# Moving the norm factor, the low parts of tile 0 and the state stores at the seams of a ConvFFN phase

## The chip, the cores and the metric

The kernel runs on one core of one Trainium2 chip. The metric is device time in microseconds (us) of one launch; lower is better. TensorE (PE in the rows) multiplies, VectorE (DVE), ScalarE (ACT) and GpSimd (POOL) work element by element, and SyncE (SP) issues every DMA of this kernel.

## What is computed

One inference step of a two-layer causal trunk, for a prompt of 1024 tokens and 8 samples of 4 tokens (T = 1056 columns together), with D = 1024, all in float32. Layer 0 mixes by convolutions, layer 1 by dilated attention; each is followed by the same ConvFFN, twice in all, and the change is in that phase:

```
def conv_ffn(h, st, w_in, wc, w_down):          # h is RMS-normed; D_FF = 2816
    z = h @ w_in                                # 1024 -> 2 * 2816: gate | up
    g, st_new = causal_dwconv(z[..., :D_FF], st, wc)   # width 3
    return (jax.nn.silu(g) * z[..., D_FF:]) @ w_down, st_new
```

The norm factor of a token (1 over the root of its mean square) is not put in the activations before the product: it is a row `rst` of T numbers by which results are multiplied later. The small conv states of layer 0 (`pa_st`, `pb_st`, `AS`, `BS`) are outputs too.

## The kernel before

**Numbers in two parts.** A float32 operand is split in a high part (a copy in fp32r, made by ScalarE) and a low part (the rest, a subtraction); each product is three matmuls (high by high, high by low, low by high). Weights arrive in `w_raw` (three slots of 1024 columns) by `load_unit` from SP.

**The products phase** (`products`, line 942 on; `ffn` of each engine) has 22 tiles j of 128 channels. A tile works on a 2 by 2 block of weights A11, A12 (unit x = 0) and A21, A22 (unit x = 1) with the sums S1 to S4, so that 11 products of 12 matmuls (L950) give gate and up. In TensorE's order they are P1 (A11), G3A, U3A (A21), P5 (S1), P2 (A12), G3B, P6 (S2), P3 (S4), P7 (S3), U3B (A22) and P4. Eight quads of 512 columns (A11, A21, S1, A12, S2, S4, S3, A22) must have both parts in a ring `wq` of six places. Per tile:
- VectorE makes the sums S (`quad_sum`, L2015 to L2023), ScalarE the high parts (`quad_hi`, L1267), GpSimd the low parts (`quad_lo`, L1682);
- ScalarE copies three half-made results out of PSUM (`copy_part` 0, 1, 2, L1281), after P1, P5 and P6; P6, P3 and P7 wait for copies 0, 1 and 2. Copy 1 of tile j also waits for `hidden(j-1)`, whose input it overwrites;
- VectorE adds the pieces (`combine` 0 to 3, L2034 to L2048; the last after P7), scales the gate (`scale_gate`), does the conv (`taps`), ScalarE `silu`, and VectorE `hidden(j)`: three multiplications of up by `sil` (L2094), which stand at the start of tile j+1 and release `prod_ok`.

**The order of queues** is written out by hand and each engine works strictly in it. SP in tile j: `store_hid(j-1)`, which waits for the last of the three multiplications and writes the row to DRAM (`hid_spill`); then `load(base+2*j+3)`, the unit with A21 and A22 of tile j+1; then `load(base+2*j+4)`, with A11 and A12 of tile j+2; in layer 1 and some tiles of layer 0 a 4 MB cache copy. ScalarE in tile j: copy 0, S3, A22, copy 1, A11 and A21 of tile j+1 (A21 waits for its load), copy 2, then S1, A12, S2, S4 of tile j+1, silu(j). GpSimd in tile j: low parts of S3, A22, then of A11, A21, S1, A12 of j+1, `history(j)`, low parts of S2, S4 of j+1; the low part of S2 waits for the sum S4, which VectorE makes after `taps`.

**The start** of the phase (tile 0) also makes the split activations `xo` while the last outputs of the mixer are added to h (L1805); the mean squares are summed in `acc`, spread by TensorE into the PSUM tile `ob`, rooted on ScalarE, and inverted on VectorE (`factor_parts`, L1787). In layer 0 SP issues all ten conv-state stores at j = 0 (L615), between two weight loads and the first hidden store.

**The end and the down phase** (`down_proj`, L806): the hidden rows come back from DRAM in pairs g of 11 (`load_hid`, L595, into `hraw`), GpSimd multiplies each by `rst` (`hidden_scale`, L1703), ScalarE makes the high part (L1478), VectorE the low one (`hidden_lo`, L2099), and TensorE multiplies; two PSUM regions alternate, and VectorE adds each to h. For g+1 both `hidden_lo` stand after the fourth of the eight additions of g.

Of the kernel before, what the change touches and what calls it, by code (L numbers as in the profile page):

```python
# [24 lines left out]
ALU = mybir.AluOpType  # L25
# [168 lines left out]
def build(nc, xT, wstream, par, ident_d, ones_d, stA, stB, stF, kva, kvb, wtab, sbias, cache_k, cache_v,  # L194
# [3 lines left out]
    with ExitStack() as ctx:  # L198
# [41 lines left out]
        AS0 = off  # L240
# [20 lines left out]
        wqr, _ = place("wqr", [P, 6, 2, 512], F32, W1)  # L261

# [38 lines left out]
        ZU = (reg[0][:, 2, 0:TS], ob[:, 1, 0:TS])  # L301

# [55 lines left out]
        hid_out = [sem(f"hid_out{i}") for i in range(2)]  # L358
        hid_in = [sem(f"hid_in{i}") for i in range(2)]
        hr_ok = sem("hr_ok")  # L360
# [33 lines left out]
        def slot_free(eng, L, j, q):  # L394


            n = 8 * j + q
            if n >= 6:
                jj, qq = divmod(n - 6, 8)
                eng.wait_ge(step_full, step_at(L, jj, LAST_STEP[qq]))  # L400
            else:
                for u in range(U_FFN[L] - 3, U_FFN[L]):
                    if u % 3 == ring(L, j, q) // 2:
                        eng.wait_ge(full, LAST[u] + 1)

# [39 lines left out]
        def load_unit(sp, u, slot, i=None, step=3):  # L445

            v = u - 3
            if is_in_unit(v):
# [3 lines left out]
                sp.wait_ge(wq_lo, 8 * (NJ * L + j) + (Q_A22 if x else Q_A12) + 1)  # L452
# [76 lines left out]
        def _(sp):  # L529
# [42 lines left out]
            def ffn_stream(L, last_unit, copies):  # L572
# [8 lines left out]
                def store_hid(j):  # L581
                    sp.wait_ge(prod_ok, 3 * (NJ * L + j + 1))
                    sp.dma_start(hid_d[j], stage[j % 2][:]).then_inc(hid_out[j % 2], 16)

                def load_hid(g):
                    if g >= NG:
                        return
                    for c in range(2):
                        sp.wait_ge(hid_out[c], 16 * (NG * L + g + 1))
# [12 lines left out]
                for j in range(NJ):  # L602
                    if j > 0:
                        store_hid(j - 1)
                    load(base + 2 * j + 3)
                    if j == NJ - 1:
                        load_hid(0)
                    load(base + 2 * j + 4)
                    if L == 0 and j == 0:
# [4 lines left out]
                        for dst, src in states:  # L614
                            sp.dma_start(dst, src).then_inc(st_out, 16)  # L615
# [115 lines left out]
        def _(pe):  # L731
# [203 lines left out]
            def products(L, j):  # L935
# [7 lines left out]
                def product(q, o, out, first, ready):  # L943
                    pe.wait_ge(wq_lo, 8 * jj + q + 1)
# [18 lines left out]
                if j >= 2:  # L963
                    pe.wait_ge(prod_ok, 3 * (jj - 2) + 2)
                product(Q_A21, X_B13, zu, True, lambda k: 3 * k + 2)
# [4 lines left out]
                product(Q_S1, X_T1, ZB, True, lambda k: 3 * k + 3)  # L970
                if j == 0:
# [4 lines left out]
                product(Q_A12, X_B21, ZC, True, lambda k: 12 + 2 * k + 1)  # L976
                product(Q_A12, X_B23, ZG, False, lambda k: 12 + 2 * k + 2)
                if j == 0:
                    pe.wait_ge(std_ok, n - 1)
                    nc.tensor.matmul(ob[:, 0, 0:NS], ones[:, :], acc[:, NP_:], start=True, stop=True).then_inc(st_full, 1)  # L980
# [10 lines left out]
            def ffn(L):  # L991
# [3 lines left out]
                for g in range(NG):  # L995
                    pe.wait_ge(hid_lo, NJ * L + 2 * g + 2)
                    for x in range(2):
                        u = down_unit(L, g, x)
                        down_proj(u, FIRST[u], g % 2, turn=(lambda: pe.wait_ge(prod_ok, 3 * NJ * (L + 1))) if g + x == 0 else None)
# [222 lines left out]
        def _(act):  # L1222
# [28 lines left out]
            def x_sum_hi(L, o, n):  # L1251

                act.wait_ge(xo_raw, 7 * L + n)
                nc.scalar.activation(xo[:, o, 0, :, :], xraw[:, o, 1, :, :], ACT.Copy).then_inc(xo_hi, 1)

            def quad_hi(L, j, q):

                jj = NJ * L + j
                if q in SUM_AT:
                    act.wait_ge(wq_raw, 4 * jj + SUM_AT[q])  # L1260
                    src = wqr[:, ring(L, j, q), 1, :]
                else:
# [20 lines left out]
            def first_tiles(L):  # L1283

                s = (1, 3)[L]
                for m in range(KD):
                    if m % 2 == 0 or L == 1:
                        hi_after(act, U_OUT + 4 + m // 2 if L == 0 else U_WO + m)
                    h_ready(act, s, m)
                    square(s, m, h[:, m, :])  # L1290
                    x_tile(L, m)
                    if m >= 5:
                        quad_hi(L, 0, (Q_A11, Q_A21, Q_S1)[m - 5])
# [6 lines left out]
                x_sum_hi(L, X_T3, 5)  # L1300
# [1201 lines left out]
```

## Time and profile before

| | us |
|---|---|
| median of 3 runs | 2687.76 (2686.51 to 2688.47) |
| the profiled execution: its own time | 2687.0 |
| its span, first to last instruction | 2685.2 |
| TensorE busy (share) | 2546.3 (95%) |
| VectorE, ScalarE, GpSimd busy | 1665.7, 811.9, 957.0 |
| mean granted TensorE clock | 0.983 of full speed |

Busy times are sums over the span; an engine's idle time counts only where TensorE then waits. The products phase of layer 0 runs from 376 to 870 us, its down phase from 881 to 1156; in layer 1 they are at 1888 to 2374 and 2385 to 2660.

### The profile page before, as it was taken

Reading aid. Unit: us, or ns where it says so; the run is one execution under the profiler, and the core shown is the slowest. Engines: PE = TensorE matmul, PEld = TensorE weight load, DVE = VectorE, ACT = ScalarE, POOL = GpSimd, SP = SyncE. Lnnn points to the kernel's source line nnn. Section 1 sums busy time; section 2 is a strip of 40 time slices with the busy share of each in tenths; the row PEclk is TensorE's granted clock in tenths of the full one; section 3 lists DMA queues with packets and bytes.
Section 4 is the critical chain, followed back from the end, with each engine's and each line's share of the span. In section 5 each row is a group of like instructions: output and inputs, shape, how many; then the busy total and the mean of one; then the engine's idle time right before and its main releaser. Section 6 shows DMA issues by size and latency. Waiting matters only on the chain.

```text
span 2685.2 us, 41621 instructions
## 1 busy us (share of the span) xinstructions
PE 2546.3 (95%) x17036; PEld 2381.7 (89%) x17036; DVE 1665.7 (62%) x2577; ACT 811.9 (30%) x1396; POOL 957.0 (36%) x651
## 2 busy tenths in 40 slices
PE   8999987999999899999999999989799999989997
PEld 8999977999999899997777777769799999989997
DVE  6999675655556555565555555554766555566555
ACT  5111342333333111143333333342433333321112
POOL 1000135555565444340001101133455555544442
PEclk9999999999999899999999999999899999989998
DMA  4111107334434344434444344442187777754221
GB/s 148 48 32 48 43 8 73 134 134 150 142 135 176 139 147 148 145 151 153 138 146 162 128 171 145 162 144 74 32 297 276 275 268 279 286 191 160 88 80 65
DMA packets 106557, 383.93 MB, mean 143 GB/s; under 512 B 23936, under 2 KB 41216, under 8 KB 103936
## 3 DMA queue, kind: packets, MB, share of 16 engines
q1 hardware_dynamic: 106368, 381.26, 42.3%
q8 instruction: 136, 2.23, 0.3%
q14 instruction: 53, 0.43, 0.1%
HBM read 339.15 MB, written 176.04 MB: 192 GB/s over the span
## 4 chain that ended last, share of the span: by engine, by line
PE 83%; DVE 11%; issue 2%; ACT 1%; POOL 1%; DMA 1%; DVEq 0%; SPq 0%; ACTq 0%
PE reg L950 29%; PE reg L806 15%; PE reg L753 11%; PE reg L1062 9%; PE ob L950 3%; PE reg L879 3%; PE reg L1042 3%; PE ob L1098 3%; DVE hid L2099 2%; DVE h L1805 2%; PE reg L1015 1%; PE reg L1083 1%; PE ob L1083 1%; PE reg L1151 1%; DVE xo L1995 1%
## 5 line engine op out<-in xcount | busy, mean ns | idle before, releaser
L950 PE MATMUL reg<-xo,wq 128*128 128x352 f32 x5280 | 863.8, 324 | 27.6 <-ACT g L1281 21.0
L950 PEld LDWEIGHTS reg<-xo,wq 128*128 128x128 f32 x5280 | 852.0, 190 | 32.7 <-ACT g L1281 22.9
L806 PE MATMUL reg<-hid,w_sp 128*128 128x352 f32 x3150 | 521.1, 327 | 48.2 <-DVE h L1805 27.9
L806 PEld LDWEIGHTS reg<-hid,w_sp 128*128 128x128 f32 x3150 | 514.7, 191 | 54.6 <-DVE h L1805 33.7
L1805 DVE TENSOR_TENSOR h<-reg,h 128x1056 f32<-128x1056 f32 x199 | 249.8, 1255 | 274.7 <-PE reg L806 220.5
L470 POOL TENSOR_TENSOR w_sp<-w_raw,w_sp 128x1024 fp32r<-128x1024 f32 x63 | 175.1, 2780 | 679.7 <-ACT w_sp L465 659.3
L1682 POOL TENSOR_TENSOR wq<-wqr,wq 128x512 fp32r<-128x512 f32 x176 | 229.4, 1313 | 353.9 <-DVE wqr L2023 215.5
L753 PE MATMUL reg<-xs,w_sp 128*128 128x352 f32 x1872 | 308.9, 326 | 10.1 <-DVE xs L1794 9.7
L753 PEld LDWEIGHTS reg<-xs,w_sp 128*128 128x128 f32 x1872 | 304.6, 189 | 13.2 <-issue 12.8
L1062 PE MATMUL reg<-xs,w_sp 128*128 128x352 f32 x1512 | 279.5, 332 | 0.4 <-DVE VT L2205 0.4
L1682 POOL TENSOR_TENSOR wq<-w_raw,wq 128x512 fp32r<-128x512 f32 x176 | 254.2, 1455 | 53.1 <-ACT wq L1267 53.1
L1062 PEld LDWEIGHTS reg<-xs,w_sp 128*128 128x128 f32 x1512 | 240.6, 188 | 18.1 <-issue 18.1
L1267 ACT ACTIVATE wq<-wqr 128x512 fp32r<-128x512 f32 x176 | 111.3, 632 | 435.0 <-DVE wqr L2023 190.7
L488 POOL TENSOR_TENSOR w_sp<-w_raw,w_sp 128x1024 fp32r<-128x1024 f32 x21 | 49.9, 2376 | 475.9 <-ACT w_sp L483 457.2
L465 ACT ACTIVATE w_sp<-w_raw 128x1024 fp32r<-128x1024 f32 x83 | 87.8, 1057 | 414.6 <-PE reg L806 255.8
L1267 ACT ACTIVATE wq<-w_raw 128x512 fp32r<-128x512 f32 x176 | 109.9, 625 | 146.2 <-PE reg L950 97.1
L1554 ACT ACTIVATE pT<-ob 128x512 f32<-128x512 f32 (+1 forms) x96 | 47.1, 491 | 329.3 <-PE ob L1083 329.3
L2069 DVE SCALAR_TENSOR_TENSOR acc<-g,pt,acc 128x1024 f32<-128x1024 f32 x88 | 121.1, 1376 | 3.1
L1703 POOL TENSOR_TENSOR hraw<-hraw,rst 128x1056 f32<-128x1056 f32 x44 | 112.1, 2569 | 27.7 <-DMA hraw<-hid_spill 27.7
L2246 DVE COPY pT<-reg 128x512 f32<-128x512 f32 (+1 forms) x96 | 53.4, 556 | 97.8 <-PE reg L1083 97.4
L2223 DVE CUSTOM_DVE_ANT_0 neg_s<-reg,wt 128x512 f32<-128x512 f32 (+1 forms) x192 | 107.2, 558 | 6.6
L1547 ACT ACTIVATE neg_s<-neg_s,nmx 128x896 f32<-128x896 f32 (+7 forms) x128 | 98.1, 768 | 35.6 <-DVE nmx L2228 33.0
(244 smaller groups left out, 2911.5 us busy)
## 6 DMA issues: line engine op xcount, KB each, us to landing
w_raw<-in_wstream SPq DMA_DIRECT2D x192, 512.0 KB, 3.8
out_sv<-in_cache_v SPq DMA_DIRECT2D x16, 4088.0 KB, 15.2
out_sk<-in_cache_k SPq DMA_DIRECT2D x16, 4088.0 KB, 15.4
kvr<-in_kva SPq DMA_DIRECT2D x16, 2048.0 KB, 8.9
kvr<-in_kvb SPq DMA_DIRECT2D x16, 1536.0 KB, 7.1
hraw<-hid_spill SPq DMA_DIRECT2D x44, 528.0 KB, 4.5
hid_spill<-tmp SPq DMA_DIRECT2D x22, 528.0 KB, 2.9
hid_spill<-stage SPq DMA_DIRECT2D x22, 528.0 KB, 2.9
```

The lines of the kernel that those rows point to most:

```text
L470: nc.gpsimd.tensor_tensor(w_sp[:, u % 3, 1, :], w_raw[:, u % 3, :], w_sp[:, u % 3, 0, :].bitcast(F32), ALU.subtract).then_inc(w_lo, 1)
L753: mm = nc.tensor.matmul(out[:, t, :], w[:, wh, k * P:(k + 1) * P], xs[:, xh, k, t * TS:(t + 1) * TS], start=(n == 0 and wh + xh == 0), sto ...
L806: mm = nc.tensor.matmul(out[:, t, :], w[:, wh, kk * 512 + m * P:kk * 512 + (m + 1) * P], hid[:, par_g, kk, xh, t * TS:(t + 1) * TS], start ...
L950: mm = nc.tensor.matmul(out, w[:, wh, k * P:(k + 1) * P], xo[:, o, xh, k, :], start=(first and k == 0 and wh + xh == 0), stop=(k == 3 and ...
L1062: mm = nc.tensor.matmul(dense[:, t, :], w[:, wh, k * P:(k + 1) * P], xs[:, xh, k, t * TS:(t + 1) * TS], start=(k == 0 and wh + xh == 0), s ...
L1267: nc.scalar.activation(wq[:, ring(L, j, q), 0, :], src, ACT.Copy).then_inc(wq_hi, 1)
L1547: nc.scalar.activation(neg_s[:, hh, 0:w], neg_s[:, hh, 0:w], ACT.Exp, bias=nmx[:, m, hh:hh + 1], scale=-1.0, accum_out=lsum[:, 0, hh:hh + ...
L1682: nc.gpsimd.tensor_tensor(wq[:, r, 1, :], src, wq[:, r, 0, :].bitcast(F32), ALU.subtract).then_inc(wq_lo, 1)
L1703: nc.gpsimd.tensor_tensor(x, x, rst[:, :], ALU.mult).then_inc(hr_ok, 1)
L1805: nc.vector.tensor_tensor(tok(h[:, m, :]), region(r), tok(h[:, m, :]), ALU.add).then_inc(free, 1)
L2069: chain(nc.vector.scalar_tensor_tensor(out=y, in0=g, scalar=w[k], in1=y, op0=ALU.mult, op1=ALU.add))
L2223: nc.vector.tensor_tensor_reduce(out=neg_s[:, hh, lo:lo + w], in0=S[hh][:, 0:w], in1=wt[:, hh, t0:t0 + w], scale=-1.0, scalar=3.0e38, op0= ...
```

## The change

1. The norm factor: `hidden_scale` is gone. GpSimd has `silu_scale(j)`, a multiplication of the silu tile by `rst` (128x1056, in place), placed in tile j+1 after the low parts of S3 and A22; `hidden(j)` waits for it. One tile `tmp` holds the result instead of two, with one semaphore `hid_out`. `quad_sum(j, S3)` stands ahead of `hidden(j-1)`.
2. The low parts of tile 0's eight quads are made by VectorE (`quad_low`, `quad0_lo`); its first six quads have other ring places, free earlier; the T2 sum is written into T4's raw rows.
3. The sum of the sample tokens has a PSUM place of its own (`z_sample`), and the sums are multiplied after G3B.
4. The ten state stores are issued one a tile, in tiles 3 to 12, behind the loads.
5. In the last tile ScalarE copies the last up results out of PSUM (`last_copy`), so that the down phase need not wait for the last hidden row; `hidden(21)` goes behind two additions of the down phase, `load_hid(0)` ahead of a weight load, and the two `hidden_lo` of g+1 are set apart, after additions 4 and 6.

```diff
 def store_hid(j):
     sp.wait_ge(prod_ok, 3 * (NJ * L + j + 1))
-    sp.dma_start(hid_d[j], stage[j % 2][:]).then_inc(hid_out[j % 2], 16)
+    sp.dma_start(hid_d[j], tmp[:]).then_inc(hid_out, 16)
...
 for j in range(NJ):
     if j > 0:
         store_hid(j - 1)
-    load(base + 2 * j + 3)
     if j == NJ - 1:
         load_hid(0)
+    load(base + 2 * j + 3)
     load(base + 2 * j + 4)
-    if L == 0 and j == 0:
+    if L == 0 and j == 3:
...
-        for dst, src in states:
-            sp.dma_start(dst, src).then_inc(st_out, 16)
+    if L == 0 and 3 <= j < 3 + len(states):
+        dst, src = states[j - 3]
+        sp.dma_start(dst, src).then_inc(st_out, 16)
...
+def silu_scale(j):
+    pool.wait_ge(silu_ok, NJ * L + j + 1)
+    nc.gpsimd.tensor_tensor(sil[:, PAD:], sil[:, PAD:], rst[:, :], ALU.mult).then_inc(silr_ok, 1)
...
 for j in range(NJ):
-    quad_lo(L, j, Q_S3)
-    quad_lo(L, j, Q_A22)
+    if j > 0:
+        quad_lo(L, j, Q_S3)
+        quad_lo(L, j, Q_A22)
+        silu_scale(j - 1)
     if j < NJ - 1:
         for q in (Q_A11, Q_A21, Q_S1, Q_A12):
             quad_lo(L, j + 1, q)
...
         split_lo(pool, down_unit(L, 0, 0))
         history(j)
+        silu_scale(j)
         split_lo(pool, down_unit(L, 0, 1))
-        hidden_scale(0)
         split_lo(pool, down_unit(L, 1, 0))
...
 def hidden(j):
-    jj, out = J0 + j, stage[j % 2]
-    dve.wait_ge(silu_ok, jj + 1)
-    dve.wait_ge(step_full, step_at(L, j, STEP_P4))
-    if jj == 1:
-        dve.wait_ge(st_out, 16 * (2 + 2 * CA))
-    if jj >= 2:
-        dve.wait_ge(hid_out[j % 2], 16 * (jj // 2))
+    jj = J0 + j
+    dve.wait_ge(silr_ok, jj + 1)
...
+    if jj >= 1:
+        dve.wait_ge(hid_out, 16 * jj)
...
 for j in range(NJ):
     more = j < NJ - 1
     if j > 0:
+        quad_sum(j, Q_S3)
         hidden(j - 1)
-        quad_sum(j, Q_S3)
     combine(j, 0)
...
+    if not more:
+        hidden_lo(0, 0)
     combine(j, 3)
...
-hidden_lo(0)
-hidden(NJ - 1)
-hidden_lo(1)
 for g in range(NG - 1):
     for x in range(2):
         for m in range(4):
             add_to_h(FIRST[down_unit(L, g, x)] + m, 4 * x + m)
-        if x == 0 and 1 <= g and g + 1 < NG:
-            hidden_lo(g + 1)
+            if g == 0 and x == 0 and m == 1:
+                hidden(NJ - 1)
+            if (x, m) in ((0, 3), (1, 1)):
+                hidden_lo(g + 1, x)
```

## Rows read from the trace of the kernel before

**Rows 1.** The page's costliest groups: two of TensorE's (busy, mean ns | idle before).

```profile
L950 PE MATMUL reg<-xo,wq 128*128 128x352 f32 x5280 | 863.8, 324 | 27.6 <-ACT g L1281 21.0
L806 PE MATMUL reg<-hid,w_sp 128*128 128x352 f32 x3150 | 521.1, 327 | 48.2 <-DVE h L1805 27.9
```

**Rows 2.** Windows: length, busy PE, PEld, DVE, ACT, POOL, granted clock, DMA share, GB/s.

```profile
449.00:855.00 406.00, 406.00 (x2557) 406.00 (x2556) 234.44 (x368) 134.32 (x231) 232.43 (x211) 1.00 0.40 137
```

**Rows 3.** Timeline, around one tile's start in layer 0: start, length, engine, work [idle before].

```profile
635.97 0.52 DVE L2048 TENSOR_TENSOR u<-reg,u 128x352 f32<-128x352 f32 x1 [0.34 <-PE reg L950]
...
642.88 0.63 ACT L1267 ACTIVATE wq<-wqr 128x512 fp32r<-128x512 f32 x1 [4.13 <-DVE wqr L2023]
642.99 2.54 POOL L1682 TENSOR_TENSOR wq<-wqr,wq 128x512 fp32r<-128x512 f32 x2 [4.86 <-DVE wqr L2023]
...
644.52 0.96 DVE L2094 TENSOR_TENSOR tmp<-reg,sil 128x352 f32<-128x352 f32 x2 [1.68 <-ACT sil L1466]
...
645.95 0.33 SPq L583 DMA_DIRECT2D hid_spill<-tmp  x1
646.55 3.66 SPq L458 DMA_DIRECT2D w_raw<-in_wstream  x2
...
647.26 1.30 POOL L1682 TENSOR_TENSOR wq<-wqr,wq 128x512 fp32r<-128x512 f32 x1 [1.73 <-ACT wq L1267]
...
648.51 2.55 POOL L1682 TENSOR_TENSOR wq<-w_raw,wq 128x512 fp32r<-128x512 f32 x2
...
651.23 0.63 ACT L1267 ACTIVATE wq<-w_raw 128x512 fp32r<-128x512 f32 x1 [2.65 <-PE reg L950]
...
653.13 0.47 ACT L1281 ACTIVATE g<-reg 128x352 f32<-128x352 f32 x1 [1.27 <-PE reg L950]
...
656.95 0.53 DVE L2048 TENSOR_TENSOR u<-reg,u 128x352 f32<-128x352 f32 x1 [0.34 <-PE reg L950]
```

**Rows 4.** The GpSimd multiplication by rst, and all loads of L458: issue to landing.

```profile
L1703 POOL TENSOR_TENSOR hraw<-hraw,rst x44: 2451/2477/3387, 870.8 to 2620.7; 128x1056 f32<-128x1056 f32 x44
...
DMA to landing us min/median/max: 3.3/3.6/14.8
```

**Rows 5.** Timeline, tile 1: the A21 load and copy, in both layers.

```profile
441.81 0.63 ACT L1267 ACTIVATE wq<-w_raw 128x512 fp32r<-128x512 f32 x1 [8.11 <-DMA w_raw<-in_wstream]
...
442.85 3.89 PE L950 MATMUL reg<-xo,wq 128*128 128x352 f32 x12 [7.13 <-ACT g L1281]
...
1942.74 3.61 SPq L458 DMA_DIRECT2D w_raw<-in_wstream  x2
...
1947.49 0.63 ACT L1267 ACTIVATE wq<-w_raw 128x512 fp32r<-128x512 f32 x1 [2.73 <-DMA w_raw<-in_wstream]
...
1948.53 2.58 PE L950 MATMUL reg<-xo,wq 128*128 128x352 f32 x12 [0.34 <-ACT g L1281]
```

**Rows 6.** Timeline, first product of each phase, and a state store of layer 0.

```profile
376.13 4.08 PE L950 MATMUL reg<-xo,wq 128*128 128x352 f32 x24
...
420.18 5.59 SPq L615 DMA_DIRECT2D out_sB<-BS  x1
...
1887.61 6.36 PE L950 MATMUL reg<-xo,wq 128*128 128x352 f32 x36 [0.66 <-issue]
```

**Rows 7.** Timeline, last product and start of the down phase, layer 0.

```profile
868.39 2.07 PE L950 MATMUL reg<-xo,wq 128*128 128x352 f32 x12
...
880.61 7.79 PE L806 MATMUL reg<-hid,w_sp 128*128 128x352 f32 x36 [10.15 <-issue]
...
891.49 36.55 PE L806 MATMUL reg<-hid,w_sp 128*128 128x352 f32 x216 [3.09 <-DVE h L1805]
...
929.28 23.48 PE L806 MATMUL reg<-hid,w_sp 128*128 128x352 f32 x144 [1.24 <-DVE h L1805]
```

**Rows 8.** Timeline, VectorE in the down phase of layer 0, beside GpSimd.

```profile
881.50 1.62 DVE L2094 TENSOR_TENSOR stage<-u,sil 128x352 f32<-128x352 f32 x1
...
923.44 4.62 DVE L2099 TENSOR_TENSOR hid<-hraw,hid 128x1056 fp32r<-128x1056 f32 x2
```

More of the change, by code:

```diff
@@ L357, in build @@
         part_ok, comb_ok, gate_n, prod_ok = (sem(s) for s in ("part_ok", "comb_ok", "gate_n", "prod_ok"))
-        hid_out = [sem(f"hid_out{i}") for i in range(2)]
+        hid_out, quad0_lo, last_up = sem("hid_out"), sem("quad0_lo"), sem("last_up")
         hid_in = [sem(f"hid_in{i}") for i in range(2)]
-        hr_ok = sem("hr_ok")
         q_ok, ss_full, ss_free = sem("q_ok"), sem("ss_full"), sem("ss_free")
@@ L404, in slot_free, with quad_ready, quad_src @@
                         eng.wait_ge(full, LAST[u] + 1)
+        def quad_ready(eng, L, j, q):
+            if j == 0:
+                eng.wait_ge(quad0_lo, 8 * L + q + 1)
+            else:
+                eng.wait_ge(wq_lo, 8 * ((NJ - 1) * L + j - 1) + q + 1)
+        def quad_src(L, j, q):
+            if q in SUM_AT:
+                return wqr[:, ring(L, j, q), 1, :]
+            return raw_half(L, j, q in (Q_A21, Q_A22), q in (Q_A12, Q_A22))
         def raw_landed(eng, u):
@@ L587, in load_hid @@
                         return
-                    for c in range(2):
-                        sp.wait_ge(hid_out[c], 16 * (NG * L + g + 1))
+                    sp.wait_ge(hid_out, 16 * (NJ * L + 2 * g + 2))
                     if g < 2:
@@ L970, in products @@
                 product(Q_S1, X_T1, ZB, True, lambda k: 3 * k + 3)
+                product(Q_A12, X_B21, ZC, True, lambda k: 12 + 2 * k + 1)
+                product(Q_A12, X_B23, ZG, False, lambda k: 12 + 2 * k + 2)
                 if j == 0:
@@ L975, in products @@
                     mm.then_inc(st_full, 1)
[L976 to L980, printed above, removed]
+                    nc.tensor.matmul(z_sample, ones[:, :], acc[:, NP_:], start=True, stop=True).then_inc(st_full, 1)
                 pe.wait_ge(part_ok, 3 * jj + 1)
@@ L1489, in ffn @@
                             quad_hi(L, j + 1, Q_A21)
-                    copy_part(L, j, 2)
+                        else:
+                            down_hi(0)
+                        copy_part(L, j, 2)
                     if more:
@@ L2105, in ffn @@
                     add_to_h(A_USE[m] if L == 0 else FIRST[U_WO + m], m)
+                    if m == 5:
+                        quad_low(Q_A11)
+                        quad_low(Q_A21)
+                    if m == 6 and L == 1:
+                        quad_sum(0, Q_S1)
                     if m == KD - 1:
-                        quad_sum(0, Q_S1)
+                        quad_low(Q_S1)
                     if m < 4:
@@ L2121, in ffn @@
                             x_lo_part(X_B23, x, 2, 12 + 2 * (x - 4) + 2)
+                        if m == 5 and L == 0:
+                            quad_sum(0, Q_S1)
                 for m in range(KD - 2, KD):
@@ L2132, in ffn @@
                 for k in range(4):
-                    ins = nc.vector.scalar_tensor_tensor(out=xraw[:, X_T2, 1, k, :], in0=third(h[:, k, :], 0), scalar=gain(k),
+                    ins = nc.vector.scalar_tensor_tensor(out=xraw[:, X_T4, 1, k, :], in0=third(h[:, k, :], 0), scalar=gain(k),
                                                          in1=xraw[:, X_T3, 1, k, :], op0=ALU.mult, op1=ALU.subtract)
@@ L2165, in ffn @@
                         quad_sum(j + 1, Q_S2)
+                    else:
+                        hidden_lo(0, 1)
                     if j == 0:
                         factor_parts((5, 9)[L])
+                        quad_sum(1, Q_S4)
                         scale_gate(0)
                     taps(j)
-                    if more:
+                    if more and j > 0:
                         quad_sum(j + 1, Q_S4)
-                hidden_lo(0)
-                hidden(NJ - 1)
-                hidden_lo(1)
                 for g in range(NG - 1):
```

140 lines of the change are left out of this document (78 added, 62 removed).

## Prediction

> **What bounds the kernel now.** I read the page first. TensorE is busy for nearly the whole span, and the waits in front of its two FFN lines are 27.6 and 48.2 us [rows 1]: that is all that a change at the seams can take away, with the clock lost beside it. Then the windows: between the seams, in the products phase, TensorE is busy for 406.00 of 406.00 us at a granted clock of 1.00, the 2.4 GHz level, while VectorE has 234 and GpSimd 232 us of work [rows 2]. So a middle tile has nothing to win, only something to lose, and the question is how far its other engines can be delayed. The timeline of one tile answers it. Its period, from one combine 3 to the next, is 656.95 - 635.97 = 20.98 us [rows 3], 11 products of 1.91 us. The seams are read last [rows 5 to 8].
>
> **Part 1, the norm factor in the middle tiles.** The count of multiplications stays at 44; only the place moves. In place of a stretch where GpSimd waited for DMA, it now stands between silu and the hidden row, in GpSimd's queue behind two low parts. What queues behind the hidden row decides. SP waits for it in `store_hid(j-1)` and only then issues the load that brings A21 of the next tile. ScalarE copies A21 ahead of copy 2, and P7 waits for copy 2. Today this is hidden: the load goes out at 646.55, A21 is copied at 651.23, released by TensorE and not by the DMA, and copy 2 stands at 653.13, when P6 has ended [rows 3]; P7 can start 1.9 us after P6. After the change a closed chain runs from the combine 3 of one tile to that of the next. Its terms:
> - combine 3 to the high copy of S4, over the sums, the gate and the taps: 642.88 - 635.97 = 6.91 us [rows 3].
> - On GpSimd: 0.11 lag, low parts of S2 and S4 2.54, of S3 and A22 2.55 (as the pair at 648.51), then the multiplication 2.48 (the median) [rows 3, 4]: 7.68. ScalarE and `quad_sum(S3)`, now earlier, keep ahead of these.
> - The hidden row, 644.52 to 645.92, with a lag of 0.05: 1.45. The store 0.03 later, the load right behind it: I put 0.4 for the issue, an estimate over the store's own 0.33 [rows 3]. Together 1.88.
> - Load to landing. All loads: 3.3 at least, 3.6 at the median [rows 4]. Behind a hidden store it is longer: 1947.49 - 1942.74 = 4.75 [rows 5]; and 4.68 from 646.55 to 651.23 was enough [rows 3]. I take 4.2, between the median and these.
> - A21's copy, copy 2, first matmul of P7: 442.85 - 441.81 = 1.04 [rows 5]. P7 itself 1.91. P7's end to combine 3: 0.34 [rows 3].
> The sum is 6.91 + 7.68 + 1.88 + 4.20 + 1.04 + 1.91 + 0.34 = 23.96 us, 2.98 over 20.98. The chain, not TensorE, becomes the bound of the middle tiles, with a wait of some 3 us in front of each P7. Copy 1 also waits for the hidden row now and releases P3 just in time, about 16.9 us after P7 of the tile before against 9 products, 17.2: no second loss, unless the row is late.
>
> **The clock** makes it dearer. After a wait of 3.09 us, 216 matmuls took 36.55, where 144 take 23.48 after a wait of 1.24 [rows 7], so 216 would take 35.2: 1.3 lost. After 7.13 us of waiting P7 took 3.89 instead of 2.07 [rows 5, 7], half speed, the 1.2 GHz level. A slow P7 stands in the chain. Bounds are 0 and 1.8 a tile; I take 0.8, as the nearest row by length of wait lost something, but over 216 matmuls. That is 3.8 a tile.
>
> How many tiles: the chain closes from P7 of tile 1 to P7 of tile 20, 19 periods in a layer, 38 in all (tile 21 has no A21 of a next tile). 38 x 3.8 = 144 us slower. Bounds of the rate: with 3.3 of landing and a full clock 2.1, so 80 us; with 4.8 of landing, 1.8 of clock and 0.5 of contention 5.9, so 224 us.
>
> A rule on contention speaks against this place too. The third multiplication of the hidden row reads two SBUF tensors; beside a GpSimd instruction it took 1.62 instead of 0.52 us [rows 8]; the lag of some 0.4 us, when A11's low part starts with the hidden row, is in the upper bound and not in the sum. The Trainium skill, page "SBUF — State Buffer", section "SBUF: two separate sides", has the rule: the port pair that VectorE and GpSimd share is an exclusive lock, held for a whole instruction. By that rule the row would come late by the rest of GpSimd's low part in each tile, and the sum would be 0.4 x 38 = 15 us higher.
>
> **Part 2, low parts of tile 0, the ring places and the T2 rows; part 3, the sums; part 4, the state stores.** From the first product to P7 of tile 1 layer 0 takes 442.85 - 376.13 = 66.7 us, layer 1 1948.53 - 1887.61 = 60.9 [rows 5, 6]. The difference of 5.8 is the state stores, issued ahead of the weight load with up to 5.59 us of SP's time for one [rows 6]: part 4 gains it. Spread over ten tiles, each goes out behind the weight loads with 20 us until the next store: I cost them at nothing; if that cover is gone, the next load lands some us later and lengthens the chain. Parts 2 and 3 bring the conv of tile 0 forward by some 5 us, by my tracing of the queues, as waits for GpSimd's low parts and for the root go. But P7 of tile 1 again stands behind the hidden row of tile 0, which now comes after two low parts and the multiplication: 2.55 + 2.48 = 5.0 later. The two cancel; bounds -3 and +5 a layer. So 6 us are gained here.
>
> **Part 5, the end of the products and the down phase.** The last product ends at 870.46, the down phase begins at 880.61, a wait of 10.15 [rows 7], as `hidden_scale`, the high part and the low part follow the taps on busy queues. After the change the pair 0 needs no multiplication; its row of tile 20 is stored later, though, its load lands at about the end of P7, and P4 of tile 21 then waits for combine 3 behind `hidden_lo(0, 0)`. I trace 2 us of wait in all, so 8.2 less. From 880.61 to 928.04 there are 252 matmuls in 47.4 us; at 23.48 for 144 they take 41.1: 6.3 less, as the 3.09 us wait and the slow clock go. 14.5 a layer, 29 in both; bounds 14 and 33. The last hidden row moves behind two additions, under 11.6 us of matmuls of the first unit.
> In each further g TensorE waits 1.24 us because two low parts of 4.62 us together stand between additions [rows 7, 8]. One of them moved takes off 2.3 at the mean, more than the wait. 9 in a layer, 18 in all: 22 us, with 15 as the lower bound where the one left is the one slowed by GpSimd.
>
> **The sum.** 144 - 6 - 29 - 22 = +87. Against the profiled execution (its own time 2687.0, span 2685.2, so 1.8 around it) that is 2774; the median of the runs, 2687.76, is 0.8 higher, and I forecast 2774.
>
> **The rivals.**
> - *The chain stays hidden: faster.* It decides from a period of 20.98 on: if GpSimd, the landing and the sums together were 3.0 us quicker than their rows, P7 would not wait, and only the gains remain, 57 us: 2631. Against it: 2.48 for the multiplication and two low parts of 1.3 are a floor. For it: a queue order may let something go ahead that I did not see. Chance 0.12.
> - *The clock falls in every tile.* 3.0 + 1.8 = 4.8, 182 us, less 57: 2813. For it: TensorE stands still for 3 us in each period, as ahead of 891.49. Against it: nothing fell after 1.24 us. 0.23.
> - *The chain closes, but is short:* loads land in 3.3 and the clock holds, 2.1 a tile: 80 - 57, 2711. For it the minimum of the landings; against it the store ahead of each load. 0.17.
> - *The gains outweigh or the change does nothing in all:* 2687 within noise, 0.02.
> My forecast, a rate of 3 to 4.5 a tile: 0.46.
>
> **How the numbers follow.** The measurement can tell about 0.2%, 5 us. Faster 0.12, same 0.02, slower 0.86. The range reaches from the short chain less the upper gains, 2700, to the falling clock with long landings, 2850; the hidden case lies outside it.
>
> **What would show it.** Right: in the middle tiles TensorE waits 3 us or so in front of P7, 38 times, released by ScalarE's copy (line of `copy_part`), and ScalarE ahead of it waits for the DMA of `w_raw`; the window of the middle tiles has TensorE at some 87% instead of 100%; the issue of the load stands 6 us later after silu. The waits of 1.24 in the down phase are gone, and the gap of 10.15 is about 2. Wrong: a middle tile of 20.98 us; then the forecast fails by its largest term. A period under 23 would show the landing or the clock overdrawn.

## The result, and the profile of the changed kernel

The changed kernel takes 2813.52 us (median of 4 runs, 2812.15 to 2817.45), against 2687.65 for the kernel before, run beside it: a ratio of 1.0471, 95% interval 1.0453 to 1.0489. It is 126 us slower, where 87 were forecast. The span grew from 2685.2 to 2812.1, and the mean granted clock fell from 0.983 to 0.967.

The two groups that answer to [rows 1], from the page:

```profile
L964 PE MATMUL reg<-xo,wq 128*128 128x352 f32 x5280 | 923.8, 337 | 155.4 <-ACT g L1293 129.5
L820 PE MATMUL reg<-hid,w_sp 128*128 128x352 f32 x3150 | 510.0, 323 | 0.7 <-DVE h L1826 0.7
```

The ledger can be read off already. In the products the idle time went from 27.6 to 155.4 us, and TensorE's own time from 863.8 to 923.8: the same 5280 matmuls, each slower at the mean. In the down phase the idle time fell from 48.2 to 0.7 and the busy time from 521.1 to 510.0. So +127.8 and +60.0, less 47.5 and 11.1: +129.2, beside the 126.9 by which the span grew. So the down phase gained about what was expected, and the products lost over three times as much.

The wait has one releaser, as the waits of TensorE show (releaser, total us, count, longest):

```profile
PE reg L964 <- ACT g L1293: 129.5, 42, 5.9
```

Of the 42 waits 40 stand ahead of P7, in tiles 1 to 20 of each layer (2.96 us at the mean); the other two (5.26 and 5.92) stand ahead of P6 of tile 1, which waits for copy 0, and come with the start. The stretch of the middle tiles, and one of the down phase, against the 406.00 of 406.00 of [rows 2]:

```profile
440.00:900.00 460.00, 403.91 (x2372) 397.29 (x2371) 219.98 (x342) 122.51 (x216) 261.19 (x217) 0.95 0.34 112
930.00:1160.00 230.00, 226.30 (x1392) 225.46 (x1391) 127.83 (x113) 47.39 (x51) 67.34 (x31) 0.99 0.45 156
```

TensorE is busy for 88% of the first stretch, at a granted clock of 0.95. VectorE, ScalarE and GpSimd are all far from full: no engine is the bound there. The timeline of one tile, to be read beside [rows 3], shows what is:

```profile
620.19 0.53 DVE L2078 TENSOR_TENSOR u<-reg,u 128x352 f32<-128x352 f32 x1 [1.91 <-PE reg L964]
...
626.89 0.63 ACT L1279 ACTIVATE wq<-wqr 128x512 fp32r<-128x512 f32 x1 [4.13 <-DVE wqr L2044]
...
627.00 4.26 POOL L1706 TENSOR_TENSOR wq<-wqr,wq 128x512 fp32r<-128x512 f32 x3 [5.46 <-DVE wqr L2044]
...
632.47 2.05 POOL L1726 TENSOR_TENSOR sil<-sil,rst 128x1056 f32<-128x1056 f32 x1
...
634.56 0.95 DVE L2127 TENSOR_TENSOR tmp<-reg,sil 128x352 f32<-128x352 f32 x2 [5.70 <-POOL sil L1726]
...
635.97 0.33 SPq L597 DMA_DIRECT2D hid_spill<-tmp  x1
636.40 1.21 SPq L472 DMA_DIRECT2D w_raw<-in_wstream  x2
...
641.75 0.63 ACT L1279 ACTIVATE wq<-w_raw 128x512 fp32r<-128x512 f32 x1 [4.73 <-DMA w_raw<-in_wstream]
...
642.79 3.29 PE L964 MATMUL reg<-xo,wq 128*128 128x352 f32 x12 [3.43 <-ACT g L1293]
...
646.11 0.53 DVE L2078 TENSOR_TENSOR u<-reg,u 128x352 f32<-128x352 f32 x1 [1.62 <-PE reg L964]
```

It is the closed chain, link for link: combine 3 at 620.19, the high copy of S4, three low parts and one more, the multiplication (L1726), the hidden row, its store, the load right behind it, 5.35 us until A21 is copied (this time released by the DMA, where before it was released by TensorE), P7 at 642.79, combine 3 at 646.11. The period is 25.92 us where it was 20.98.

The seams, in TensorE's timeline, against [rows 5 to 7]:

```profile
375.60 7.91 PE L964 MATMUL reg<-xo,wq 128*128 128x352 f32 x48
...
437.77 3.12 PE L964 MATMUL reg<-xo,wq 128*128 128x352 f32 x12 [2.89 <-ACT g L1293]
...
924.52 9.80 PE L964 MATMUL reg<-xo,wq 128*128 128x352 f32 x60 [2.40 <-ACT g L1293]
...
953.24 3.15 PE L964 MATMUL reg<-xo,wq 128*128 128x352 f32 x12 [3.25 <-DVE u L2078]
956.19 12.40 PE L820 MATMUL reg<-hid,w_sp 128*128 128x352 f32 x72
...
1945.00 7.95 PE L964 MATMUL reg<-xo,wq 128*128 128x352 f32 x48
...
2006.21 3.89 PE L964 MATMUL reg<-xo,wq 128*128 128x352 f32 x12 [1.56 <-ACT g L1293]
...
2498.95 11.39 PE L964 MATMUL reg<-xo,wq 128*128 128x352 f32 x60 [3.47 <-ACT g L1293]
```

P7 of tile 1 stands 5.1 us earlier than before in layer 0 (437.77 against 442.85). P7 of tile 20, in layer 0, is at 924.52: 19 periods of 25.62 us; in layer 1, (2498.95 - 2006.21) / 19 = 25.93. The wait of 10.15 us ahead of the down phase has become 3.25 ahead of P4 of tile 21, and the down phase starts without one.

### The profile page after: what moved, and what is told of

Same layout as the page of the kernel before. It is cut to its first block, busy times and chain, and to the rows that moved or that the text cites. A ratio compares the mean times of both kernels' runs of the same rounds, so it can differ in the third digit from the quotient of the medians.

```text
span 2812.1 us, 41623 instructions
## 1 busy us (share of the span) xinstructions
PE 2602.9 (93%) x17036; PEld 2430.6 (86%) x17036; DVE 1617.9 (58%) x2593; ACT 804.9 (29%) x1400; POOL 919.0 (33%) x635
## 4 chain that ended last, share of the span: by engine, by line
PE 58%; DVE 15%; POOL 11%; DMA 8%; issue 5%; ACT 2%; SPq 1%; DVEq 0%; ACTq 0%; POOLq 0%
PE reg L820 18%; PE reg L767 11%; PE reg L1076 8%; POOL wq L1706 8%; DMA w_raw<-in_wstream 7%; PE reg L964 6%; DVE acc L2099 3%; POOL sil L1726 3%; PE reg L893 3%; PE reg L1056 2%; PE ob L1112 2%; DVE tmp L2127 2%; DVE wqr L2040 1%; PE reg L1029 1%; PE reg L1097 1%
## 5 line engine op out<-in xcount | busy, mean ns | idle before, releaser
L964 PE MATMUL reg<-xo,wq 128*128 128x352 f32 x5280 | 923.8, 337 | 155.4 <-ACT g L1293 129.5
L964 PEld LDWEIGHTS reg<-xo,wq 128*128 128x128 f32 x5280 | 897.0, 199 | 174.0 <-ACT g L1293 141.9
L820 PE MATMUL reg<-hid,w_sp 128*128 128x352 f32 x3150 | 510.0, 323 | 0.7 <-DVE h L1826 0.7
L1706 POOL TENSOR_TENSOR wq<-wqr,wq 128x512 fp32r<-128x512 f32 x168 | 259.1, 1561 | 223.8 <-DVE wqr L2044 212.7
L1706 POOL TENSOR_TENSOR wq<-w_raw,wq 128x512 fp32r<-128x512 f32 x168 | 220.6, 1314 | 292.3 <-ACT wq L1279 292.3
L2127 DVE TENSOR_TENSOR tmp<-reg,sil 128x352 f32<-128x352 f32 x64 | 31.5, 522 | 248.6 <-POOL sil L1726 248.6
L2036 DVE TENSOR_TENSOR wqr<-w_raw 128x512 f32<-128x512 f32 x44 | 30.4, 692 | 181.5 <-DMA w_raw<-in_wstream 181.5
L2099 DVE SCALAR_TENSOR_TENSOR acc<-g,pt,acc 128x1024 f32<-128x1024 f32 x88 | 115.1, 1308 | 3.1
```

The source lines that it names most:

```text
L820: mm = nc.tensor.matmul(out[:, t, :], w[:, wh, kk * 512 + m * P:kk * 512 + (m + 1) * P], hid[:, par_g, kk, xh, t * TS:(t + 1) * TS], start ...
L964: mm = nc.tensor.matmul(out, w[:, wh, k * P:(k + 1) * P], xo[:, o, xh, k, :], start=(first and k == 0 and wh + xh == 0), stop=(k == 3 and ...
L1706: nc.gpsimd.tensor_tensor(wq[:, r, 1, :], quad_src(L, j, q), wq[:, r, 0, :].bitcast(F32), ALU.subtract).then_inc(wq_lo, 1)
L2099: chain(nc.vector.scalar_tensor_tensor(out=y, in0=g, scalar=w[k], in1=y, op0=ALU.mult, op1=ALU.add))
L2127: nc.vector.tensor_tensor(third(tmp, t), u, third(sil[:, PAD:], t), ALU.mult).then_inc(prod_ok, 1)
```

## The experiments

All ratios are to the kernel before, run beside it on the same chip. Not all experiments ran on one chip (its medians there were 2690.4, 2694.9 and 2692.0), so kernels from different chips are compared by their ratios. Five experiments on the changed kernel come first.

**Twice the multiplication.** It is the cheapest test of whether GpSimd's time is in the chain. The output holds the norm factor twice.

```diff
     nc.gpsimd.tensor_tensor(sil[:, PAD:], sil[:, PAD:], rst[:, :], ALU.mult).then_inc(silx_ok, 1)
+    pool.wait_ge(silx_ok, NJ * L + j + 1)
+    nc.gpsimd.tensor_tensor(sil[:, PAD:], sil[:, PAD:], rst[:, :], ALU.mult).then_inc(silr_ok, 1)
```

> The changed kernel with the multiplication by the norm factor done twice in a row on GpSimd (the output then holds that factor twice). Theory A: every term of GpSimd in front of the hidden row counts in full, so 2.05 us and a hand-over of some 0.1 in each of 38 periods: 82 us more, 2895 (2880 to 2910). Theory B, contention: VectorE waits for the hidden row anyway and has nothing running beside it, so 2813 to 2840.

Measured: 2918.3, ratio 1.0852 [1.0816, 1.0889], slightly above the range of the chain theory and far from that of contention. Against the ratio of the changed kernel it is 0.038 more, 102 us, or 2.4 for each of 42 tiles. The second multiplication begins 2.13 later than the first:

```profile
651.78 2.06 POOL L1727 TENSOR_TENSOR sil<-sil,rst 128x1056 f32<-128x1056 f32 x1
...
653.91 2.06 POOL L1729 TENSOR_TENSOR sil<-sil,rst 128x1056 f32<-128x1056 f32 x1
```

Over the middle tiles the multiplication ends 2.0 us later behind combine 3, and the period is 28.1 us where it was 25.7. So a microsecond of GpSimd is a microsecond of the tile and a little more; the remaining 0.4 stands between P7's start and combine 3, which is clock (3.57 us against 3.14, at a granted clock of 0.957 at the mean). P3 now waits for copy 1 too, in all 42 tiles, 56.4 us in all, but inside the same period.

**The load ahead of the store.** This cuts the chain at the link between the hidden row and the load, and changes nothing on GpSimd.

```diff
+    load(base + 2 * j + 3)
-    if j > 0:
-        store_hid(j - 1)
     if j == NJ - 1:
         load_hid(0)
-    load(base + 2 * j + 3)
     load(base + 2 * j + 4)
+    if j > 0:
+        store_hid(j - 1)
```

> The changed kernel (2813.5) with one edit in SP's queue: in each tile both weight loads are issued ahead of the hidden store. Theory A, the chain: the middle tiles last 25.8 us because the load of A21 waits behind the store of the hidden row; the load now goes out some 9 us earlier, the chain is cut, only copy 1 (released by the hidden row) is left, at 20.7 us by its terms, so the period is 20.98 again, the 182 us of the 38 tiles come back and the kernel takes about 2630 (2620 to 2650), faster than the kernel before by the seams alone. Theory B, contention: the multiplication on GpSimd slows VectorE in the middle tiles wherever it stands, and the order of DMAs has no part: 2800 or more. Theory C, half of it: copy 1 and P3 take the place of copy 2 and P7 as the thing that waits, with a period of 21.5 to 22.5: 2650 to 2690.

Measured: 2652.4 (2648.8 to 2652.5), ratio 0.9864 [0.984, 0.9888]. One store moved behind two loads, and the kernel went from 4.7% slower than before to 1.4% faster. The waits ahead of P7 are gone in tiles 1 to 20, and the period is 21.7, not 20.98. That is theory C, by the second path that the prediction had as just in time: copy 1 waits for the hidden row, and P3 for copy 1.

```profile
562.91 0.46 ACT L1293 ACTIVATE u<-reg 128x352 f32<-128x352 f32 x1 [6.00 <-DVE tmp L2127]
563.43 4.08 PE L964 MATMUL reg<-xo,wq 128*128 128x352 f32 x24 [0.49 <-ACT u L1293]
...
585.16 11.71 PE L964 MATMUL reg<-xo,wq 128*128 128x352 f32 x72 [0.48 <-ACT u L1293]
```

**The multiplication first.** GpSimd scales silu ahead of the low parts of S3 and A22.

```diff
     if j > 0:
+        silu_scale(j - 1)
         quad_lo(L, j, Q_S3)
         quad_lo(L, j, Q_A22)
-        silu_scale(j - 1)
```

> The changed kernel with one edit in GpSimd's queue: the multiplication by the norm factor stands ahead of the low parts of S3 and A22. Theory A: the hidden row comes 2.57 us earlier, the chain is shorter by that, a period of about 23.2 and, with less clock lost, 2690 to 2725; TensorE's waits ahead of P7 are below 1.5 us. Theory B, contention: no gain, or some us either way: 2800 to 2830.

Measured: 2697.9, ratio 1.0039 [1.0022, 1.0056]. The chain stays closed and is shorter by one and a half low parts: the multiplication ends some 2 us earlier after combine 3 (12.7 against 14.8 at the mean), and the period is 22.9. P7 still waits some 1.4 us in each tile, but mostly runs at full speed:

```profile
618.85 2.20 PE L964 MATMUL reg<-xo,wq 128*128 128x352 f32 x12 [1.63 <-ACT g L1293]
...
641.80 9.81 PE L964 MATMUL reg<-xo,wq 128*128 128x352 f32 x60 [1.43 <-ACT g L1293]
```

The 12 matmuls take 2.20, and the next 60 take 9.81 in a row, 1.96 a dozen. From P7's start to combine 3 it is 2.2 to 2.4 us in 34 of the 38 periods. So a wait of some 1.4 us in each tile left the granted clock at the 2.4 GHz level in most of them, and 2 us off the chain gave back 2.8, the other 0.8 between P7's start and combine 3 (3.14 to 2.33).

**Copy 2 ahead of A21's copy.** ScalarE's order was one link of the chain; here P7 need not wait behind the load.

```diff
     if more:
         quad_hi(L, j + 1, Q_A11)
+    copy_part(L, j, 2)
+    if more:
         quad_hi(L, j + 1, Q_A21)
     else:
         down_hi(0)
-    copy_part(L, j, 2)
```

> The changed kernel with one edit in ScalarE's queue: copy 2 stands ahead of A21's high part. Theory A: P7 no longer waits for the load, but VectorE's sum S1 of the next tile still does, ahead of combine 2, the gate and combine 3, for which P4 waits; landing to combine 3 is then 2.3 to 3.4 us instead of 4.36, so a period of 24 to 24.8 and 2740 to 2775, with the wait of TensorE in front of P4 and not of P7. If the high part of A21 alone were the link: 2630. Theory B: 2813 unchanged.

Measured: 2785.5, ratio 1.0359 [1.0326, 1.0391], 10 us above the range. The direction is right and the size is not: only about 30 us of 126 came back. The wait did not go; it moved from P7 two products down, to P4, and a part of it stands ahead of P3, which waits for copy 1 and so for the hidden row.

```profile
PE reg L964 <- DVE u L2079: 81.4, 42, 3.3
PE reg L964 <- ACT u L1293: 52.9, 31, 3.2
```

P4 now waits for combine 3, 42 times, since VectorE makes the sum S1 of the next tile ahead of combine 3, and S1 needs the same load:

```profile
659.51 0.69 DVE L2037 TENSOR_TENSOR wqr<-w_raw 128x512 f32<-128x512 f32 x1 [4.19 <-DMA w_raw<-in_wstream]
...
662.15 0.51 DVE L2079 TENSOR_TENSOR u<-reg,u 128x352 f32<-128x352 f32 x1
```

The load closes the chain over two engines. To take it out of one queue is not enough.

**The loads apart.** Is the landing, 4.9 us at the mean against the 4.2 of the prediction, the work of the second load, issued 0.4 us behind the first? Here SP waits until the first has landed.

```diff
     load(base + 2 * j + 3)
+    if 0 < j < NJ - 1:
+        sp.wait_ge(w_in[(base + 2 * j + 3) % 3], slot_cnt(base + 2 * j + 3))
     load(base + 2 * j + 4)
```

> The changed kernel, with SP waiting for the first load of a tile to land before it issues the second. In the changed kernel the load of A21 took 4.9 us to land in its middle tiles, against 4.2 in my sum and 3.6 at the median before. Theory 1: the second load, issued 0.4 us later, takes part of the rate; apart, A21 lands in 4.3 or less and the period falls by 0.6, 2790 (2780 to 2800). Theory 2: the store of the hidden row 0.43 us ahead is what lengthens it, and nothing changes: 2813, landing 4.7 to 4.9.

Measured: 2783.0, ratio 1.0336 [1.0295, 1.0378], 0.0135 under the changed kernel, 36 us by the ratios; the two profiled spans differ by 28.7. Over the 38 periods the time from the issue to A21's copy is 4.37 at the mean instead of 4.89, and the period 25.00 instead of 25.72. In a middle tile:

```profile
656.86 4.45 SPq L472 DMA_DIRECT2D w_raw<-in_wstream  x2
...
661.04 0.63 ACT L1281 ACTIVATE wq<-w_raw 128x512 fp32r<-128x512 f32 x1 [3.55 <-DMA w_raw<-in_wstream]
```

Of the 0.7 a tile that came back, 0.5 is the landing and 0.3 stands in P7, whose start to combine 3 fell from 3.14 to 2.84; 0.1 was lost again ahead of the hidden row.

**Both orders.** The load ahead of the store, and the multiplication first. This takes away both paths on which the hidden row comes late; what is left is what the change gains at the seams.

```diff
+    load(base + 2 * j + 3)
-    if j > 0:
-        store_hid(j - 1)
...
     load(base + 2 * j + 4)
+    if j > 0:
+        store_hid(j - 1)
...
+        silu_scale(j - 1)
         quad_lo(L, j, Q_S3)
         quad_lo(L, j, Q_A22)
-        silu_scale(j - 1)
```

> The changed kernel with both edits, the loads ahead of the hidden store and the multiplication ahead of the low parts of S3 and A22. After the first edit alone P3 still waited 0.48 us in each middle tile for copy 1, which waits for the hidden row (period 21.75). Theory A': that is a second chain through copy 1, of the same GpSimd terms; 2.57 us less in it brings the period to 20.98, TensorE waits nowhere in a middle tile, and the kernel takes 2652 - 38 x 0.77 = 2623 (2618 to 2630). Rival: the 0.77 us are a cost of GpSimd's and VectorE's work side by side, and stay: 2645 to 2655.

Measured: 2614.2 (2609.7 to 2621.1), ratio 0.9712 [0.9682, 0.9742]. This version beats both kernels: 2.9% faster than before, 7.2% faster than the change as it was made. The chain through copy 1 is gone as expected; the time is 4 us under the range that was given, since that counted the middle tiles alone (they gave 22.5 of the 39.1 us between the two spans) and not the start, which gave another 10.0. The middle tiles are nearly full again:

```profile
440.00:860.00 420.00, 417.53 (x2620) 416.95 (x2620) 274.15 (x375) 138.44 (x241) 294.86 (x237) 1.00 0.47 144
```

The down phase of layer 0 begins at 859.29 (880.61 before), the products of layer 1 at 1847.25 (1887.61), and the span ends at 2607.9 (2685.2): 21.3, 40.4 and 77.3 us ahead. The four experiments that follow undo one part of the change at the seams each, in this version, where nothing downstream swallows it.

**The low parts of the hidden pair together again.**

```diff
-            if (x, m) in ((0, 3), (1, 1)):
-                hidden_lo(g + 1, x)
+            if (x, m) == (0, 3):
+                hidden_lo(g + 1, 0)
+                hidden_lo(g + 1, 1)
```

> As the run with both orders, but both hidden low parts of g+1 stand together behind the fourth addition, as in the kernel before. My theory of the down phase: VectorE then holds back the fifth addition and TensorE waits about 1.2 us in each of 9 or 10 groups a layer, 22 us more than the run with both orders (18 to 28). Rival: the waits were there because GpSimd's multiplications of the hidden rows slowed the low parts, and are gone with them: 0 to 5 us more.

Measured: 2640.9, ratio 0.9808 [0.9783, 0.9833], 26.7 us more on the same chip. The waits of the down phase are back, 20 of them, though GpSimd no longer multiplies hidden rows:

```profile
PE reg L820 <- DVE h L1826: 25.3, 20, 1.5
```

Each down phase is longer by 13.4 us. So it was the two low parts in a row that held the additions, and not GpSimd's multiplication beside them.

**The ten state stores at once, in tile 0.**

```diff
-    if L == 0 and 3 <= j < 3 + len(states):
-        dst, src = states[j - 3]
-        sp.dma_start(dst, src).then_inc(st_out, 16)
+    if L == 0 and j == 0:
+        for dst, src in states:
+            sp.dma_start(dst, src).then_inc(st_out, 16)
```

> As the run with both orders, but the ten conv-state stores are issued at once in tile 0, as in the kernel before. In the kernel before they cost layer 0 5.8 us against layer 1. Here the loads of tile 1 also stand behind them: 5 to 12 us more. Rival: with the loads no longer in a chain they are hidden: 0 to 2 us more.

Measured: 2624.2, ratio 0.975 [0.9719, 0.9781], 10 us more on the same chip, with intervals that overlap. The trace settles it: the load behind the last store goes out at 424.00, and P7 of tile 1 waits, so that layer 0 takes 9.1 us longer from its first product to combine 3 of tile 1:

```profile
416.13 4.69 SPq L628 DMA_DIRECT2D out_sB<-BS  x1
424.00 5.81 SPq L472 DMA_DIRECT2D w_raw<-in_wstream  x2
```

```profile
438.20 3.89 PE L963 MATMUL reg<-xo,wq 128*128 128x352 f32 x12 [6.36 <-ACT g L1292]
```

It also shows the other side of part 4. From there to combine 3 of tile 20 layer 0 takes 399.95 us, against 402.89 with the stores spread over tiles 3 to 12. There, in two tiles, a state store and a 4 MB cache copy stand ahead of the loads, the load of A21 lands 9.4 and 11.5 us after its issue, and the tiles take 21.96 and 22.76 us; with the stores at once the same two tiles take 20.98.

**The low parts of tile 0 on GpSimd again.** The eight calls move from VectorE's start to GpSimd's, three of them among the squares, five behind them.

```diff
+    if m >= 5:
+        quad_low0(L, (Q_A11, Q_A21, Q_S1)[m - 5])
+for q in (Q_A12, Q_S2, Q_S4, Q_S3, Q_A22):
+    quad_low0(L, q)
...
-    quad_low(Q_A11)
-    quad_low(Q_A21)
```

> As the run with both orders, but GpSimd makes the eight low parts of tile 0, as in the kernel before, at the same points of the order. In my forecast parts 2 and 3 gained nothing, since the hidden row of tile 0 held P7 of tile 1 back again; with both orders changed that no longer holds. If the move to VectorE is worth the waits for GpSimd's low parts (2.07 and 0.86 us and the longer activations' low parts in the kernel before): 5 to 12 us more than the run with both orders, for both layers. If VectorE is just as late with them: within 3 us.

Measured: 2625.5, ratio 0.9752 [0.9731, 0.9773]; 0.0040 over the version that it changes, 11 us; the two intervals just touch. TensorE waits for GpSimd five times, 10.0 us in all, in tile 0 of the two layers; the three of layer 0:

```profile
375.83 4.08 PE L964 MATMUL reg<-xo,wq 128*128 128x352 f32 x24
380.61 2.19 PE L964 MATMUL reg<-xo,wq 128*128 128x352 f32 x12 [0.69 <-POOL wq L1729]
...
395.19 4.06 PE L964 MATMUL reg<-xo,wq 128*128 128x352 f32 x24 [2.44 <-POOL wq L1729]
...
402.35 6.78 PE L964 MATMUL reg<-xo,wq 128*128 128x352 f32 x24 [3.11 <-POOL wq L1729]
```

From the first product to U3B of tile 1 it is 61.2 us in both layers (375.83 to 437.04 in layer 0), against 56.6 with VectorE's low parts: 4.6 a layer. ScalarE and VectorE keep the order of the changed kernel here, so this prices the low parts alone, not parts 2 and 3 together.

**The last hidden row ahead of the first addition.**

```diff
+hidden(NJ - 1)
 for g in range(NG - 1):
...
-            if g == 0 and x == 0 and m == 1:
-                hidden(NJ - 1)
```

> As the run with both orders, but VectorE makes the last hidden row ahead of the first addition of the down phase, not behind the second. The row comes about 7 us after the down phase begins, and additions 1 and 2 stand behind it, so TensorE stops after two outputs (5.8 us) and waits some 3 to 5 us, with a slow clock after: 4 to 7 us a layer, 8 to 14 in all. If the end of the phase owed its gain to something else: no change.

Measured: 2629.9, ratio 0.9761 [0.9738, 0.9785], 0.0049 more, 13 us; the two intervals just touch, and the down phases are longer by 8.1 and 7.5 us in the traces. Each layer gets one wait of 7.1 us, and what stood in its place was 1.5:

```profile
864.33 5.95 PE L820 MATMUL reg<-hid,w_sp 128*128 128x352 f32 x36
...
877.35 22.86 PE L820 MATMUL reg<-hid,w_sp 128*128 128x352 f32 x125 [7.08 <-DVE h L1826]
```

The same place with the row behind two additions (both orders):

```profile
859.29 11.76 PE L820 MATMUL reg<-hid,w_sp 128*128 128x352 f32 x72
...
872.54 27.66 PE L820 MATMUL reg<-hid,w_sp 128*128 128x352 f32 x170 [1.49 <-DVE h L1826]
```

## Why the prediction was right in kind and short in size

**The mechanism stands.** The prediction's chain is the one in the timeline above, with its wait ahead of P7, ScalarE released by the DMA, and TensorE at 88% where 87 was said. Lengthening it by a multiplication of 2.1 made the tile longer by 2.4, and cutting it at one link removed the loss altogether. The rival that the chain stays hidden falls, though its mechanism came in sight: with GpSimd 2 us quicker and the load free of the row, its number (2631) was even passed.

**The terms of the chain.** Means over the 38 periods, from combine 3, beside the forecast:

| term | forecast | measured |
|---|---|---|
| combine 3 to the end of the multiplication | 6.91 + 7.68 = 14.59 | 14.77 |
| hidden row, store, issue of the load | 1.88 | 1.88 |
| issue to A21's copy (landing) | 4.20 | 4.89 |
| A21's copy to P7 | 1.04 | 1.04 |
| P7 to combine 3, clock included | 2.25 + 0.8 = 3.05 | 3.14 |
| period | 24.76 | 25.72 |

The forecast period was too short by 1.0 us, and 38 of them are nearly the whole miss: the middle tiles grew by 179 us where 144 were put, 35 of the 40 by which the span's growth of 126.9 exceeds 87. The seams were forecast at -57 and came to -52.

**The term that was mis-sized is the landing,** put at 4.20 and measured at 4.89, which is 0.7 of the 1.0. "I take 4.2, between the median and these" was right for the kernel before: there the loads of A21 behind a hidden store land 4.18 us after their issue at the mean of the 38 middle tiles. (Of the two rows that the prediction set beside it, 4.75 was a real wait for the DMA, in a tile 1; 4.68 was not, as TensorE released that copy, and this load had landed after 4.13.) What the prediction left out is that the change moves the neighbour too. In the kernel before, the next load goes out 3.3 us behind A21's, as its slot waits for GpSimd's low part of A22; in [rows 3] the two issues span 3.66 us. In the changed kernel that low part is made ahead of the multiplication, and nothing holds the load any more when SP comes to it: the two issues span 1.21 us in the timeline above, the second 0.5 behind the first, and A21's load lands after 4.81. Holding the second load back brought the term from 4.89 to 4.37, so 0.5 of the 0.7 is shown to be that neighbour; the other 0.2 was not taken apart.

**The first term was right by two errors.** The multiplication took 2.05, not 2.48, while the low parts took longer (three in 4.26, where 1.3 each had been put); 14.59 were forecast and 14.77 came. The rest of that term is a contention that the prediction had in its upper bound only, and in another place. Here is VectorE after a P7 at full speed and after a slow one, with GpSimd's low part beside the first:

```profile
746.42 0.52 DVE L2078 TENSOR_TENSOR u<-reg,u 128x352 f32<-128x352 f32 x1 [0.53 <-PE reg L964]
...
747.63 1.67 DVE L2041 TENSOR_TENSOR wqr<-wqr,w_raw 128x512 f32<-128x512 f32 x1
...
773.37 0.53 DVE L2078 TENSOR_TENSOR u<-reg,u 128x352 f32<-128x352 f32 x1 [2.07 <-PE reg L964]
...
774.53 0.69 DVE L2041 TENSOR_TENSOR wqr<-wqr,w_raw 128x512 f32<-128x512 f32 x1
```

```profile
747.01 1.74 POOL L1706 TENSOR_TENSOR wq<-w_raw,wq 128x512 fp32r<-128x512 f32 x1
...
772.40 1.28 POOL L1706 TENSOR_TENSOR wq<-w_raw,wq 128x512 fp32r<-128x512 f32 x1
```

The sum takes 1.67 while a low part runs to 748.75, and 0.69 when it starts after that low part has ended. (The first low part is itself long, 1.74 against 1.28; VectorE's sum ahead of this one runs beside its start.) GpSimd's finish then lies 15.4 or 14.3 us behind combine 3, and the tiles alternate between the two. The third hidden product, in which the prediction had seen 0.4 us of this, took 0.52 in the middle tiles: nothing. (It took 0.73 once the multiplication stood first on GpSimd.) The rule of the Trainium skill, page "SBUF — State Buffer", section "SBUF: two separate sides", that the second comer is shut out for the whole instruction, fits the row of 1.67 (the sum ends 0.55 us behind the low part, about the 0.69 that it takes alone), but it acted on another instruction than the one to which it was applied.

**The clock** was sized well: 0.8 was put, 0.9 came (3.14 less 2.25). But it is a mixture: in 8 of the 38 periods P7 to combine 3 takes 2.2, in the others 2.6 to 3.9. A slow P7 returns a part of its loss at once, since the next sum then meets no low part. The rival "the clock falls in every tile" gave 4.8 a tile and 2813, which is the number measured, by another composition: 0.9 of clock with 0.7 of landing and 0.2 on GpSimd's side, not 1.8 of clock. The rival of the short chain (2711) had half a point: the clock mostly holds at waits of 1.4 us, as with the multiplication first, but the loads didn't land in 3.3.

**The seams,** by stretches of the three traces, layer 0 and layer 1 (combine 3 of tile 1 and of tile 20 are the marks between start, middle and end):

| stretch | before | changed | both orders |
|---|---|---|---|
| start: first product to tile 1 | 70.65, 63.54 | 65.34, 65.13 | 56.83, 56.79 |
| middle: tile 1 to tile 20 | 399.50, 398.71 | 485.80, 491.58 | 402.89, 398.83 |
| end: tile 20 to the down phase | 34.34, 34.68 | 29.46, 29.69 | 24.22, 24.22 |
| down phase | 275.88, 276.03 | 257.08, 256.60 | 257.62, 257.61 |
| all the rest of the span | 1131.9 | 1131.4 | 1128.9 |

In the changed kernel the start gained 5.3 in layer 0 and lost 1.6 in layer 1, 3.7 in all where 6 were forecast: the hidden row of tile 0 took back what parts 2 and 3 brought, and a little more. The end gained 4.9 and 5.0 where 8.2 were forecast for each; the wait left ahead of P4, put at 2, was 3.25 and 2.37, and P4 was slow behind it. The down phases gained 18.8 and 19.4, where 6.3 + 11 were forecast. That the two low parts in a row make the waits of 1.24 is shown, and the term was 22 where undoing the move cost 26.7 us. The state stores were costed at nothing where they now stand. In the changed kernel nothing shows, as the periods of layer 0, which has them, are no longer than those of layer 1; without the chain they cost layer 0 some 3 us.

**What the price hangs on.** The prediction priced the place of the multiplication in the changed kernel's own queues, which was right for this change. The runs show that the place costs little by itself: with it first on GpSimd and the load ahead of the store the middle tile is back at 21.0 to 21.3 us in most periods.

The 77 us that the version with both orders gains on the kernel before can be read from the same table: 20.6 at the two starts, 20.6 at the two ends, 36.7 in the down phases and 3.0 elsewhere, less 3.5 in the middle. The starts are where the chain had hidden most: 6 us were forecast with the hidden row of tile 0 in the way, and 20.6 came when it was not. Of these the low parts are shown to bring 4.6 a layer. The other pieces of parts 2 and 3, and ScalarE's last copy in part 5, were not undone one by one, and their shares stay open.

## What to carry to other kernels

When an operation is put later on one engine, follow its result through every in-order queue to the next load: a store that waits for it holds each load issued behind it, and here exchanging the two was worth 6% of the kernel. A tile in which TensorE is always busy hides slack that only the queues show; write the closed path from one tile to the next as a sum, and take each term from a row with the neighbours that it will have after the change: when a queue comes late, the work that used to follow at a distance follows at once. If a chain closes, take it apart at the link that costs nothing, and look for the second path behind it: here ScalarE's copy 1 and VectorE's sum S1.

## What the runs showed of the hardware that was not expected

- The landing of a weight load depends on what stands beside it in the queue. From issue to landing, at the mean of the 38 middle tiles: 4.18 us behind a hidden store with the next load 3.3 us later (kernel before), 4.81 with the next load 0.5 us later (changed kernel), 4.29 with that load held back. Behind a state store and a cache copy of 4 MB it was 9.4 and 11.5 in two tiles of the version with both orders.
- The multiplication of a 128x1056 tile by `rst` on GpSimd takes 2.05 us on `sil`, at the median of 44, and 2.48 on `hraw` [rows 4]. Both are in place and of the same shape; why is open.

```profile
L1726 POOL TENSOR_TENSOR sil<-sil,rst x44: 2045/2055/2078, 427.3 to 2534.4; 128x1056 f32<-128x1056 f32 x44
```

- Of two instructions of VectorE and GpSimd that start together, the first kept its speed. With both orders, a low part of the hidden pair that begins 0.02 us ahead of GpSimd's takes 1.25 us, the median of its line, and GpSimd's is stretched to 3.48, where the median of that line is 2.41:

```profile
897.22 1.25 DVE L2131 TENSOR_TENSOR hid<-hraw,hid 128x1056 fp32r<-128x1056 f32 x1
```

```profile
897.24 3.48 POOL L484 TENSOR_TENSOR w_sp<-w_raw,w_sp 128x1024 fp32r<-128x1024 f32 x1 [9.22 <-ACT w_sp L479]
```

- Waits of 1.4 us at the mean in each period of 22.9 left P7 fast in 34 of 38; waits of 2.4 to 4.3, 3.0 at the mean, in each of 25.7 made 30 of 38 slow, at 0.9 us a period. The length of the wait alone does not tell: in the changed kernel a P7 was fast behind 3.00 us and another slow behind 2.35.
